# Feed-forward with 512-column matmuls over high and low activations, all up units first, down in eight banks

## The reference

```python
def swiglu(x, w_gu, w_down):
    g, u = jnp.split(x @ w_gu, 2, axis=-1)
    return (jax.nn.silu(g) * u) @ w_down
h = x + 0.5 * swiglu(rmsnorm(x, g[0]), w_ffn_gu[layer, 0], w_ffn_down[layer, 0])
```

## Time and profile before

| | |
|---|---|
| median of 3 runs | 2599.1 us (2597.75 to 2599.65) |
| span of the profiled execution | 2596.8 us, 2.3 below that median |
| TensorE busy | 2542.5 us, 21,448 passes |
| VectorE busy | 1721.9 us |
| ScalarE busy | 1196.4 us |
| HBM read | 430.47 MB, 166 GB/s over the span |
| weight load of 1 MB, issue to landing | 4.8 us |

### The profile page before, as it was taken

One profiled execution on the slowest core, in us unless ns is written; L12 is line 12 of the kernel. 1 busy time (PEld: TensorE's weight loads), 2 busy tenths in 40 slices (PEclk: granted clock), 3 DMA queues, 4 the chain that ended last, 5 costly groups with the idle time before them and its releaser, 6 DMA issues.

```text
span 2596.8 us, 50251 instructions
## 1 busy us (share of the span) xinstructions
PE 2542.5 (98%) x21448; PEld 2497.8 (96%) x21448; DVE 1721.9 (66%) x2221; ACT 1196.4 (46%) x1273; POOL 29.4 (1%) x62
## 2 busy tenths in 40 slices
PE   8999999999999999999998999999999999999998
PEld 8999999999999999999978999999999999999998
DVE  6557676576566765675577656755867657788665
ACT  5445354344434544454365434544535434544643
POOL 0000000000000000000000000000000000011000
PEclk9999999999999999999998999999999999999999
DMA  7554345445444445455433544555434554445352
GB/s 275 180 188 169 113 149 197 178 179 180 179 176 147 151 180 183 176 187 182 178 116 116 181 178 178 179 180 186 170 114 160 199 180 169 173 137 165 139 188 80
DMA packets 62677, 437.12 MB, mean 168 GB/s; under 512 B 7537, under 2 KB 8689, under 8 KB 10545
## 3 DMA queue, kind: packets, MB, share of 16 engines
q1 hardware_dynamic: 59984, 426.95, 45.7%
q0 software_dynamic: 2528, 7.74, 1.0%
HBM read 430.47 MB, written 1.05 MB: 166 GB/s over the span
## 4 chain that ended last, share of the span: by engine, by line
PE 84%; DVE 10%; ACT 4%; issue 1%; DMA 0%; SPq 0%; DVEq 0%; ACTq 0%
PE ps L679 54%; PE ps L713 19%; PE ps L697 5%; DVE w_lo L1599 3%; ACT w_hi L1173 2%; DVE x L1717 1%; DVE scratch L1658 1%; PE ps L834 1%; DVE right_lo L1652 1%; PE ps L958 1%; DVE right_hi L1649 1%; DVE left_lo L1652 1%; PE ps L981 1%; PE ps L967 1%; DVE left_hi L1649 0%
## 5 line engine op out<-in xcount | busy, mean ns | idle before, releaser
L1599 DVE TENSOR_TENSOR w_lo<-raw,w_hi 128x2048 fp32r<-128x2048 f32 x404 | 925.1, 2290 | 484.3 <-ACT w_hi L1173 484.1
L1173 ACT CAST w_hi<-raw 128x2048 fp32r<-128x2048 f32 x404 | 766.1, 1897 | 494.1 <-PE ps L713 249.2
L679 PE MATMUL ps<-right_hi,w_hi 128*128 128x256 f32 x2544 | 727.4, 286 | 6.2 <-DVE right_lo L1652 3.2
L679 PE MATMUL ps<-right_hi,w_lo 128*128 128x256 f32 x2544 | 720.4, 283 | 0.0
L679 PE MATMUL ps<-right_lo,w_hi 128*128 128x256 f32 x2544 | 720.2, 283 | 0.0
L679 PE MATMUL ps<-left_hi,w_hi 128*128 128x256 f32 x1968 | 562.8, 286 | 16.0 <-DVE left_lo L1652 13.1
L679 PE MATMUL ps<-left_hi,w_lo 128*128 128x256 f32 x1968 | 557.7, 283 | 0.0
L679 PE MATMUL ps<-left_lo,w_hi 128*128 128x256 f32 x1968 | 557.6, 283 | 0.0
L679 PEld LDWEIGHTS ps<-right_hi,w_hi 128*128 128x128 f32 x2544 | 488.5, 192 | 13.1 <-issue 4.1
L679 PEld LDWEIGHTS ps<-right_hi,w_lo 128*128 128x128 f32 x2544 | 488.7, 192 | 0.4
L679 PEld LDWEIGHTS ps<-right_lo,w_hi 128*128 128x128 f32 x2544 | 488.7, 192 | 0.0
(11 more groups left out here) (297 smaller groups left out, 3089.7 us busy)
## 6 DMA issues: line engine op xcount, KB each, us to landing
raw<-weights_dram SPq DMA_DIRECT2D x404, 1024.0 KB, 4.8
scratch<-scratch POOLq DMA_DIRECT2D x48, 64.0 KB, 1.9
raw<-weights_dram SPq DMA_DIRECT2D x2, 512.0 KB, 6.0
x<-x_t_dram SPq DMA_DIRECT2D x2, 512.0 KB, 8.1
scratch<-c_second_dram POOLq DMA_DIRECT2D x1, 1024.0 KB, 10.4
scratch<-p_t_dram POOLq DMA_DIRECT2D x4, 256.0 KB, 3.0
scratch<-mem_t_dram POOLq DMA_DIRECT2D x1, 1024.0 KB, 8.1
out_dram<-scratch SPq DMA_DIRECT2D x4, 256.0 KB, 2.5
```

The source lines that it names most:

```text
L679: last = nc.tensor.matmul(bank(e, ring)[:, half * T:(half + 1) * T], l, r, start=(k == 0 and j == 0 and half == 0), stop=(k == KC - 1 and ...
L1173: nc.scalar.copy(w_hi[:, m % SPLIT, :], raw[:, m % RAW, :]).then_inc(weights_hi, 1)
L1599: V.tensor_tensor(w_lo[:, m % SPLIT, :], raw[:, m % RAW, :], w_hi[:, m % SPLIT, :].bitcast(F32), ALU.subtract).then_inc(weights_split, 1)
```

## The change

In the feed-forward alone, and in what adjoins it:
- High and low parts of the activations lie side by side in one tensor (`left_parts`, `right_parts`), the hidden ones of up 6 to 21 in a new tensor `hidden`. One matmul with `w_hi` stationary streams 512 columns, high and low together, into the two halves of a bank; a second with `w_lo` streams the 256 high columns into the second half. The first half holds high x high, the second the two small terms.
- An up unit takes two banks (gate, up); four such pairs make the ring, all of PSUM. On the way out ScalarE copies both small halves to SBUF (`small`, 128x512), VectorE adds the large ones (`fold`), multiplies by rstd (`scaled`), and from there the steps are as before, 512 columns at a time in the first two.
- Queue order for unit j from 2 on: ScalarE small j, `w_hi` of j+3, silu j, cast j; VectorE fold j, scaled j, hidden low j-1, `w_lo` of j+3, product j.
- All 22 up units run first, then the 11 down units, one bank for each of 8 output chunks. The first down unit takes its banks in the order in which the up units free them. The others hold 512 rows x 512 columns. Before the last two down units VectorE adds the small halves to x (`fold_small`), and those two run three passes of 256 as before, into the first half alone.
- At the exit the pairs are done in the order 2, 3, 0, 1 (`LATE`), and the first projection of the next phase takes its chunks in that order (`arrival`). Two `w_lo` of the next phase stand behind them, one before.
- TensorE waits for `rstd_ready` after up 2. The hardware loops go.

```diff
-            yield up(0)
-            yield up(1)
-            for s in range(1, STEPS):
-                yield up(2 * s)
-                yield up(2 * s + 1)
-                yield rows_unit(down, 256 * (s - 1))
-            yield rows_unit(down, 256 * (STEPS - 1))
+            for j in range(HCH):
+                yield up(j)
+            yield rows_unit(down, 0)
+            for d in range(1, STEPS):
+                yield block_unit(down, *down_block(d))
...
+                def up(j, operand_ready=None, parts=False):
+                    w, e = (n0 + j) % SPLIT, e0 + j
+                    pe.wait_ge(*((first_split, 1) if parts else (weights_split, n0 + j + 1)))
+                    pe.wait_ge(bank_read, e + 1)
+                    for k in range(KC):
...
+                        for half in range(2):
+                            wc = slice(k * 256 + half * P, k * 256 + (half + 1) * P)
+                            o = ps[:, up_bank(i, j) + half, :].rearrange("p (a t) -> p a t", a=2)
+                            nc.tensor.matmul(o, w_hi[:, w, wc], XG[2][:, :, k, :], start=(k == 0), stop=False,
+                                             skip_group_check=True)
+                            last = nc.tensor.matmul(o[:, 1], w_lo[:, w, wc], XG[0][:, k, :], start=False,
+                                                    stop=(k == KC - 1), skip_group_check=True)
+                    last.then_inc(weights_used, 1)
...
+                def into(c, w, wc, j, start, folded):
+                    o = ps[:, acc_bank(i, c), :].rearrange("p (a t) -> p a t", a=2)
+                    a = hidden_parts(i, j)
+                    if not folded:
+                        nc.tensor.matmul(o, w_hi[:, w, wc], a, start=start, stop=False, skip_group_check=True)
+                        return nc.tensor.matmul(o[:, 1], w_lo[:, w, wc], a[:, 0], start=False, stop=True,
+                                                skip_group_check=True)
+                    nc.tensor.matmul(o[:, 0], w_hi[:, w, wc], a[:, 0], start=False, stop=False, skip_group_check=True)
+                    nc.tensor.matmul(o[:, 0], w_lo[:, w, wc], a[:, 0], start=False, stop=False, skip_group_check=True)
+                    return nc.tensor.matmul(o[:, 0], w_hi[:, w, wc], a[:, 1], start=False, stop=True, skip_group_check=True)
...
+                def first_down():
+                    n = n0 + HCH
+                    pe.wait_ge(weights_split, n + 1)
+                    pe.wait_ge(hidden_ready, h0 + 2)
+                    for c in sorted(range(KC), key=last_up):
+                        pe.wait_ge(bank_read, e0 + last_up(c) + 5)
...
+                up(0, xg_ready, parts=(i == 0))
+                up(1)
                 norm_sums(i)
+                up(2)
                 pe.wait_ge(rstd_ready, i + 1)
+                for j in range(3, HCH):
+                    up(j)
+                first_down()
+                for d in range(1, STEPS):
+                    down(d)
```

ScalarE's and VectorE's queues:

```diff
+                def small(j):
+                    act.wait_ge(weights_used, n0 + j + 1)
+                    act.wait_ge(bank_read, e0 + j + 4)
+                    nc.scalar.copy(FFN_SMALL, up_pair(i, j)[:, :, T:2 * T]).then_inc(small_parts, 1)
...
+                norm(i, n0 + SPLIT, first_small)
+                for j in range(HCH):
+                    if j > 1:
+                        small(j)
+                    if j:
+                        high(n0 + j + SPLIT)
+                    gate = FFN_T[j % 2][:, 0]
+                    act.wait_ge(up_scaled, h0 + j + 1)
+                    nc.scalar.activation(gate, gate, ACT.Silu).then_inc(silu_ready, 1)
+                    act.wait_ge(hidden_value, h0 + j + 1)
+                    nc.scalar.copy(hidden_parts(i, j)[:, 0], FFN_H[:, j % 2]).then_inc(hidden_hi, 1)
...
+                def fold(j):
+                    dve.wait_ge(small_parts, h0 + j + 1)
+                    V.tensor_tensor(FFN_T[j % 2], up_pair(i, j)[:, :, 0:T], FFN_SMALL, ALU.add).then_inc(bank_read, 1)
...
+                for j in range(HCH):
+                    if j > 1:
+                        fold(j)
+                    scaled(j)
+                    if j:
+                        hidden_low(j - 1)
+                        low(n0 + j + SPLIT)
+                    product(j)
...
+                for d in range(STEPS - 2):
+                    if d >= STEPS - 4:
+                        fold_small(2 if d == STEPS - 4 else 0)
+                    low(n0 + HCH + d + SPLIT)
+                for place, u in enumerate(LATE):
+                    if u == 0:
+                        dve.wait_ge(acc_ready, at(i, "acc") + 1)
+                    else:
+                        dve.wait_ge(weights_used, n0 + HCH + STEPS - (u != 1))
+                    if place == 0:
+                        dve.wait_ge(acc_folded, 2 * at(i, "acc") + 2)
+                    link(add(u, 0))
+                    next_operand(i, 2 * u, 2, 2 * place)
+                low(n0 + HCH + STEPS - 2 + SPLIT)
+                low(n0 + HCH + STEPS - 1 + SPLIT)
```

More of the change, by code:

```diff
@@ L44 @@
 SPLIT = 3
-ROUND = 4
 BANKS = 4
+MO_HIDDEN = 6
+HIDDEN_AT = 4352
+LATE = (2, 3, 0, 1)
 KINDS = {
-    "ffn": dict(units=HCH + STEPS, banks=HCH, norms=1, resid=KC, hidden=HCH, acc=3),
+    "ffn": dict(units=HCH + STEPS, banks=HCH, norms=1, resid=KC, hidden=HCH, acc=1),
     "ple": dict(units=5, banks=4, norms=1, resid=KC, ple=1),
@@ L329, in build @@
         tiny = sb("tiny", [P, 96])
+        with ExitStack() as under:
+            under.enter_context(nc.sbuf_tensor("below_hidden", [P, HIDDEN_AT], F32))
+            hidden = under.enter_context(nc.sbuf_tensor("hidden", [P, 2, HCH - MO_HIDDEN, T], F32R))
         S = sb("scratch", [P, 18176])
@@ L403, in pair_of, with hidden_parts, up_bank, up_pair @@
             return bank(e, ring).rearrange("p (c t) -> p c t", c=2)
+        def hidden_parts(i, j):
+            if j < MO_HIDDEN:
+                return operands(i)[1][2][:, :, j if j < 4 else j + 2, :]
+            return hidden[:, :, j - MO_HIDDEN, :]
+        def up_bank(i, j):
+            order = (2, 0, 1, 3)
+            if i > 0 and phases[i - 1][0] == "ple":
+                order = (0, 1, 2, 3) if at(i, "banks") % BANKS == 0 else (1, 0, 2, 3)
+            return 2 * order[j % 4]
+        def up_pair(i, j):
+            return ps[:, up_bank(i, j):up_bank(i, j) + 2, :]
+        def acc_bank(i, c):
+            first = 4 if phases[i + 1][0] == "ple" else at(i + 1, "banks") % BANKS
+            return (c - 4 + first) % 8
+        def arrival(i):
+            if i > 0 and phases[i - 1][0] == "ffn":
+                return [c for u in LATE for c in (2 * u, 2 * u + 1)]
+            return list(range(KC))
+        def acc_pair(i, u, part):
+            b = acc_bank(i, 2 * u)
+            return ps[:, b:b + 2, part * T:(part + 1) * T]
         def norm_bank(i):
@@ new lines, in down @@
+                def down(d):
+                    n = n0 + HCH + d
+                    r0, c0 = down_block(d)
+                    folded = d >= STEPS - 2
+                    pe.wait_ge(weights_split, n + 1)
+                    pe.wait_ge(hidden_ready, h0 + r0 // P + 4)
+                    if folded:
+                        pe.wait_ge(acc_folded, 2 * at(i, "acc") + d + 3 - STEPS)
+                    for c in range(c0 // P, c0 // P + 4):
+                        for k in range(4):
+                            wc = slice(k * 512 + c % 4 * P, k * 512 + (c % 4 + 1) * P)
+                            last = into(c, n % SPLIT, wc, r0 // P + k, start=False, folded=folded)
+                        if d == STEPS - 1 and c == 1:
+                            last.then_inc(acc_ready, 1)
+                    last.then_inc(weights_used, 1)
@@ L1210, in ffn @@
-                for j in range(4):
-                    up(j, n0 + j, early=(j == 0))
-                high(n0 + 4 + SPLIT)
-                if i + 1 < nphase and phases[i + 1][0] == "ple":
-                    act.wait_ge(p_loaded, 16 * (at(i, "ple") + 1))
-                    nc.scalar.copy(mo_hi[:, 4:6], PLE_P).then_inc(p_hi_ready, 1)
-                if phases[i + 2:i + 3] == [("second", 0)]:
-                    act.wait_ge(p_loaded, 16 * (at(i, "ple") + 2))
-                    nc.scalar.activation(SE_MSQ, SE_MEM, ACT.Square).then_inc(own[i + 2]["memsq"], 1)
@@ L1231, in ple @@
+                for d in range(STEPS):
+                    high(n0 + HCH + d + SPLIT)
             def ple(i):
```

212 lines of the change are left out of this document (92 added, 120 removed).

## The result

The changed kernel takes 2550.3 us (median of 4 runs, 2549.4 to 2552.8) against 2599.1: a ratio of 0.982, 95% interval 0.9805 to 0.9833. The forecast was 2538, in a range of 2518 to 2578. So it is faster by about four fifths of what was forecast: 48.8 us, not 61.4. The profiled execution took 2550.9, its span is 2549.2, 47.6 under that of before.

A forecast was written before the change was run, and what follows sets the result against it. TensorE was taken as the bound, before and after. Merged passes 52.9 us, less 7 lost at feed-forward entries, plus 15.9 at exits, less 0.4 at the start: 2599.1 - 61.4 = 2538 us, range 2518 to 2578.

The forecast's parts named there:

- The merged passes: TensorE, merged units: each step drops one pass start of 13.3 ns, paid per pass whatever its columns; 52.9 us saved.
- vanishes: Rival for merged passes: surcharge gone under long passes, a step takes 333 ns, kernel 2527 us; chance 0.17.
- per column: Rival for merged passes: surcharge goes with columns, a step saves 0 to 4.6 ns, kernel 2568 to 2586 us; chance 0.25.
- the sign by which the forecast wanted to be judged: TensorE, start to start of the 512-column pass: 0.227 us if the forecast's 13.3 ns per pass is right.
- 52.9 us: Saving from merged passes in eight feed-forwards: 3,968 steps at 13.3 ns each.
- The loop: ScalarE and VectorE, up stage: closed loop of 5.40 us, 0.15 below TensorE's 5.547, so TensorE remains the bound.
- The entry: Start of a feed-forward: weights for unit 4 ready at 11.2 us, wanted at 11.5, so hidden by 0.3.
- The banks: First down unit, waiting for its last bank pair: about 0.2 us lost, 0.7 where a gate layer follows.
- The last feed-forward: Memory's square and sums lengthen the loop by 4.3 us: 3.2 lost at once, 1.0 at the bank.
- The exit: End of each feed-forward: new pair order leaves no TensorE stop in the next unit; 15.9 us gained.
- The start: First unit or two of the kernel wait for weights: about 0.4 us of their saving lost.

The follow-up runs named there:

- three_pass: Changed kernel with each merged 512-column pass split again into two of 256 columns, all else as changed: 2586.1 us.
- grouped: Changed kernel with an up unit's passes in the order 512, 512, 256, 256 instead of 512, 256, 512, 256: 2547.7 us, 0.9817 of its before.
- copy_twice: Changed kernel with the copy out of PSUM on ScalarE made twice, one after the other: 2659.6 us.
- entry: Changed kernel with the second w_hi and w_lo cast before the silu of the first up unit: 2539.6 us, 0.9781 of the kernel before.
- chores: Changed kernel with the split of p and the memory's square and sums moved from up unit 3 to down units: 2543.8 us, ratio 0.9802.
- late_exit: Changed kernel with all four pairs of x finished behind the last down unit, as in the kernel before: 2594.8 us.
- both: Changed kernel with the edits of `entry` and `chores` together: 2533.5 us, 0.9763 of the kernel before.

## Why the prediction came out 12 us too low in time

**The merged passes: the price of a step right, its reason not shown, and too few steps at that price.** The forecast took 13.3 ns for each pass, whatever its columns. A step in the fast pace costs exactly what follows from that, 346.7 ns, and 360 with the pass put back (`three_pass`). As prices of a step, "vanishes" (333) and "per column" (355 to 360) are refuted; even the slow pace is 353.3. But the sign by which the forecast wanted to be judged is off: 0.232 us behind a 512-column pass, not 0.227. Above their columns the long pass pays 18.3 ns and the short one 8.3, where the forecast had 13.3 each, and `grouped` shows the same split between equal neighbours (0.47 and 0.23 us for two). The two errors cancel in a step, and that is luck: what makes the surcharge stays open.

By the fixed cost per matmul in the Trainium skill (TensorE: Matmul & The Clock Gate, section "Wait — 56ns, not 53.3ns?") a step would take 213.3 + 106.7 + 2 x 2.5 = 325 ns, an estimate. The trace disagrees: it pays 26.7 ns above the columns where that rule has 5.

The mis-sized term is **52.9 us**: it put all 3,968 steps at 346.7. By the unit lengths, about 1.2 us went in the slow first units, 5.4 in the up units of the first, third and fifth feed-forward, and 3.9 in the down units, most of which run at 5.600 or slower. The merge brought about 42.4. No row of the kernel before shows more than one pace, so this couldn't be read ahead.

**The loop: right.** 5.39 against 5.40; the copy 0.58 against 0.59. TensorE stayed the bound in the up stage, and `copy_twice` shows what happens above that.

**The entry: the slack of 0.3 us was not there.** The walk left out that fold 0 stands on VectorE's queue behind the w_lo of the unit before. Behind a gate layer that w_lo ends late: in the third feed-forward fold 0 runs from 578.73 to 579.41, ScalarE's next copy waits for it and starts at 579.50, and the chain of w_hi and w_lo behind the norm slips with it. Around the start of the fifth unit 0.18, 0.32 and 0.08 us were lost in the third, fifth and seventh feed-forward, from the third to the fifth unit 1.9 in the first (0.5 of it ahead of the fourth, at `rstd_ready`): 2.5 in all, 0 forecast. The greater price was the slow pace behind it, 1.8 us each in the first, third and fifth. `entry` takes the stop away, and the slow pace goes with it. Which pace follows such a stop is open, and its length doesn't tell: the stop ahead of the fifth unit was 0.08 us in the third feed-forward, with the slow pace behind it, and 0.08 in the seventh, with the fast one.

**The banks: total right, spread wrong.** Where a gate layer follows, the first down unit lost 0.76, 0.74 and 0.76 us (0.7 forecast). In the seventh it lost 0.55, in the others 0 to 0.1 (0.2 forecast): 3.1 us against 2.9. Where the up units were slow, the loop had caught up.

**The last feed-forward: 4.9 us for 4.2.** Windows of the stop at its eighth unit and of the rest of that unit, and TensorE's timeline between them:

```profile
1976.37:1979.58 3.21, 0.16 (x3) 0.01 (x1) 3.21 (x4) 0.42 (x1) 0.00 (x0) 1.00 0.01 3
1979.58:1986.70 7.12, 7.12 (x31) 6.11 (x32) 5.13 (x7) 4.43 (x7) 0.00 (x0) 0.76 0.55 166
```

```profile
1979.58 0.50 PE L807 MATMUL ps<-right,w_hi 128*128 128x512 f32 x1 [3.05 <-DVE w_lo L1690]
...
1980.38 0.40 PE L807 MATMUL ps<-right,w_hi 128*128 128x512 f32 x1
...
1981.30 0.63 PE L807 MATMUL ps<-right,w_hi 128*128 128x512 f32 x1
```

The stop is 3.2 us, to the tenth the forecast. But about a microsecond behind it the clock falls to its lower level, 1.2 GHz (the 512-column pass grows from 0.40 to 0.63), and over the unit 0.76 is granted: 7.12 us for 5.43, 1.7 more. That term was missing; the 1.0 at the bank did not come, since the loop had caught up by then. `chores` takes both out.

**The exit: right, 15.9 us.** The timelines of VectorE and TensorE at the end of the second feed-forward, where the earlier trace rows had 7.43 us to the last pass of the next unit:

```profile
538.36 0.68 DVE L1810 SCALAR_TENSOR_TENSOR x<-ps,x 128x512 f32<-128x512 f32 x1
...
537.67 0.28 PE L826 MATMUL ps<-hidden,w_hi 128*128 128x256 f32 x1
537.78 0.28 PE L761 MATMUL ps<-right,w_hi 128*128 128x256 f32 x1
...
543.41 0.28 PE L761 MATMUL ps<-right,w_hi 128*128 128x256 f32 x1
```

Only the fourth pair is added behind the last pass, and TensorE goes on without a stop: 5.74 us. At all eight exits the unit is 5.75 long, and `late_exit` shows what the order is worth.

**The rest.** The start gave 0.3 us instead of taking 0.4. Two mixers moved by 1.6 and -1.5 us besides their exits, which cancel; in the faster one the granted clock is 0.94 where it was 0.88. Sum in the spans: 42.4 - 2.5 - 3.1 - 4.9 + 0.3 = 32.2, against 32.0 read from the windows; with the exits 48, less 0.3 elsewhere: 47.6.

## What to carry to other kernels

When two closed loops differ by 3%, walk the entry with every item that stands ahead of each wait on its queue, those left over from the phase before included. Price a stop of TensorE above its length: behind one of 2 us and more the clock mostly took another 1.7 or more here, and behind one of 0.1 the whole stage could run slower. Check a mechanism by the figure that only it predicts, not by a sum that two errors can meet. And one-off work (a cast of an input, a square with its sums) belongs in the stage whose queues idle: moved from the up to the down stage it took 4.1 us out of the feed-forwards of `both` against those of `entry` (6.0 in the medians), for no instruction more.

## What the runs showed of the hardware

- Behind a stop of 1.9 us (`entry`), 2.0 (`three_pass`), 3.2 (after) and 3.4 (`late_exit`) in the stream the granted clock fell for a stretch and cost about 1.7 us each time. Neither the fall nor its price is fixed by the length of the stop: behind the 4.1 us at the banks in `copy_twice` two units of some 11.1 us took 17.0 in one feed-forward and 18.5 in another, and behind 1.9 us before a mixer in `late_exit` the clock fell in one of four exits (0.82; 1.00 in the others). Behind stops of 0.5 us (after) and 1.3 (`late_exit`) it stayed at 1.00, and so it did at the exits of the kernel before, whose stops are spread over the unit.
- The same stream of 512- and 256-column passes at the same granted clock runs at 346.7 or at 353.3 ns a step for some 100 us on end, and was seen to change only at an interruption (a stop, a plain matmul). What of the interruption decides is open: stops of equal length were followed by either. In the order of `grouped` there was only 348.3.
- From the fourth down unit on, the pair of passes takes 350.0 ns a step, in every kernel here that has it. Their moving operand comes from another tensor; whether that is the reason wasn't tried.
- What a pass takes on top of its columns depends on the passes around it. Alone, 256 columns take 120 ns (`three_pass`: 13.3 on top). Beside 512-column passes they take 115 (8.3 on top) and the 512-column pass 232 (18.3 on top), and `grouped` has 0.23 us for two of the one and 0.47 for two of the other.
